# RWKV block inverse: the 16-step substitution as one run on GpSimd instead of portions on VectorE

## What is computed

```python
    def step(state, inp):
        rt, wt, kt, vt, at, bt = inp
        sa = jnp.einsum('bhvk,bhk->bhv', state, at)
        state = state * wt[:, :, None, :] + sa[..., None] * bt[:, :, None, :] + vt[..., None] * kt[:, :, None, :]
        return state, jnp.einsum('bhvk,bhk->bhv', state, rt)
```

## Time and profile before

| | |
|---|---|
| median of 3 runs | 1715.83 us (1714.31 to 1716.86) |
| the profiled execution | 1716.01 us, span 1713.9 us |
| TensorE | 1640.9 us busy, 96% of the span |
| VectorE | 1121.7 us, 65% |
| ScalarE | 874.3 us, 51% |
| GpSimd | 769.2 us, 45% |
| mean granted TensorE clock | 0.981 of 2.4 GHz |

### The profile page before, as it was taken

One profiled execution on the slowest core, in us unless ns is written; L12 is line 12 of the kernel. 1 busy time (PEld: TensorE's weight loads), 2 busy tenths in 40 slices (PEclk: granted clock), 3 DMA queues, 4 the chain that ended last, 5 costly groups with the idle time before them and its releaser, 6 DMA issues.

```text
span 1713.9 us, 30381 instructions
## 1 busy us (share of the span) xinstructions
PE 1640.9 (96%) x11876; PEld 1272.5 (74%) x11876; DVE 1121.7 (65%) x1732; ACT 874.3 (51%) x1695; POOL 769.2 (45%) x555
## 2 busy tenths in 40 slices
PE   8999999989888888899999999999999999999997
PEld 6677777745677677688977677788888888888886
DVE  8744343435576775633687769887758866784788
ACT  5323333345425444511463467776667666656763
POOL 4210212011111112312493257968768695867771
PEclk9999999988899999999999999999999999999999
DMA  6100010001112223322302002020211202020202
GB/s 242 37 26 22 25 47 1 22 6 31 33 32 49 52 36 116 140 107 73 111 25 74 1 1 98 21 79 25 74 36 63 70 30 96 29 74 26 74 1 98
DMA packets 82842, 94.47 MB, mean 55 GB/s; under 512 B 53776, under 2 KB 56336, under 8 KB 82704
## 3 DMA queue, kind: packets, MB, share of 16 engines
q1 hardware_dynamic: 82704, 92.57, 16.8%
HBM read 82.57 MB, written 9.98 MB: 54 GB/s over the span
## 4 chain that ended last, share of the span: by engine, by line
PE 78%; DVE 11%; ACT 4%; issue 3%; DMA 2%; POOL 2%; SPq 0%; DVEq 0%; ACTq 0%; POOLq 0%
PE PS L1763 40%; PE PS L1054 8%; PE PS L969 5%; PE PS L1155 3%; PE PS L1194 2%; PE PS L1173 2%; PE PS L1719 2%; PE PS L1697 1%; PE PS L1553 1%; PE PS L1228 1%; POOL sa L917 1%; DVE xn L2382 1%; PE PS L1395 1%; PE PS L1499 1%; DMA sc_s<-a_dram 1%
## 5 line engine op out<-in xcount | busy, mean ns | idle before, releaser
L1763 PE MATMUL PS<-memr,wsp 128*128 128x512 f32 x1488 | 357.6, 391 | 1.5 <-DVE memr L2952 1.5
L1763 PEld LDWEIGHTS PS<-memr,wsp 128*128 128x128 f32 x1488 | 278.8, 188 | 63.7 <-DVE memr L2952 3.7
L932 POOL TENSOR_TENSOR wsp<-sa,wsp 128x512 fp32r<-128x512 f32 x120 | 166.3, 1390 | 167.2 <-ACT wsp L2204 167.0
L1763 PE MATMUL PS<-memr,wraw_r 128*128 128x512 f32 x744 | 180.1, 390 | 0.4 <-DVE memr L2952 0.4
L1763 PEld LDWEIGHTS PS<-memr,wraw_r 128*128 128x128 f32 x744 | 139.4, 188 | 31.1 <-DVE memr L2952 1.2
L1054 PE MATMUL PS<-xn,wsp 128*128 128x512 f32 x576 | 147.8, 403 | 2.5 <-DVE proj L2427 1.6
L1763 PE MATMUL PS<-tmp_r,wsp 128*128 128x512 f32 x564 | 147.2, 395 | 2.6 <-DVE tmp_r L2952 2.2
L2952 DVE TENSOR_TENSOR memr<-PS,memr 128x512 fp32r<-128x512 f32 x185 | 126.2, 682 | 34.3 <-ACT PS L2242 34.3
L823 POOL CAST wsp<-wraw 128x1024 fp32r<-128x1024 f32 x24 | 27.9, 1161 | 239.2 <-PE PS L1054 114.2
L2970 DVE TENSOR_TENSOR H<-PS,H 128x512 f32<-128x512 f32 x160 | 108.2, 687 | 40.3 <-PE PS L1763 24.2
L1898 ACT ACTIVATE H<-PS,mst 128x128 f32<-128x128 f32 (+3 forms) x64 | 47.5, 742 | 166.1 <-DVE mst L2511 166.1
(11 more groups left out here) (394 smaller groups left out, 3437.0 us busy)
## 6 DMA issues: line engine op xcount, KB each, us to landing
sa<-in_weights_dram SPq DMA_DIRECT2D x40, 512.0 KB, 4.0
wraw<-in_weights_dram SPq DMA_DIRECT2D x24, 512.0 KB, 3.8
sa<-in_weights_dram SPq DMA_DIRECT2D x48, 256.0 KB, 2.6
H<-in_x_dram SPq DMA_DIRECT2D x16, 512.0 KB, 7.1
sbx<-in_weights_dram SPq DMA_DIRECT2D x32, 256.0 KB, 2.6
H<-in_weights_dram SPq DMA_DIRECT2D x8, 512.0 KB, 7.5
out_dram<-sbx SPq DMA_DIRECT2D x16, 256.0 KB, 2.1
a_dram<-H SPq DMA_DIRECT2D x16, 128.0 KB, 2.5
```

What stands on the lines that cost most here:

```text
L932: nc.gpsimd.tensor_tensor(w[:, 1, :], w_source(g), w[:, 0, :].bitcast(F32), ALU.subtract).then_inc(mw_rest, 1)
L1763: last = nc.tensor.matmul(PS[:, bank_of(g), :], w[:, a, win(k)], x[:, b, :], start=(k == 0 and (a, b) == (0, 0)), stop=(k == ROWS - 1 and ...
```

## The change

Places 24 and 26 to 30 leave VectorE. GpSimd gets place 24 (two memsets) and one place 26, in which all 15 steps and the transposed copy stand in one run; each of these instructions waits for the one before it on GpSimd's own counter `P_POOL`. SP waits for xt on that counter. Shapes, operands and operations stay the same.

```diff
-SUBST = {26: (0, 1, 2, 3), 27: (4, 5, 6, 7), 28: (8, 9, 10, 11), 29: (12, 13), 30: (14,)}
+SUBSTITUTE = 26
...
         P_DVE = Steps(sem("prep_dve"), each(
-            ["kk", "t1p", "L", "na", "am", "k2", "nkk", "at", "b", "bt", "kt", "al0", "al1", "al2", "al3", "rk", "x0", "x1"]
-            + [y for place in SUBST for j in SUBST[place] for y in (f"xm{j}", f"xa{j}")] + ["xt", "bv0", "bv1a", "bv1"]))
-        P_POOL = Steps(sem("prep_pool"), each(["rt", "kh", "bh"]))
+            ["kk", "t1p", "L", "na", "am", "k2", "nkk", "at", "b", "bt", "kt", "al0", "al1", "al2", "al3", "rk", "bv0", "bv1a", "bv1"]))
+        P_POOL = Steps(sem("prep_pool"), each(
+            ["rt", "kh", "bh", "x0", "x1"] + [y for j in range(BLK - 1) for y in (f"xm{j}", f"xa{j}")] + ["xt"]))
...
-                sp.wait_ge(P_DVE.sem, P_DVE.at(f"xt_{n}", -1))
+                sp.wait_ge(P_POOL.sem, P_POOL.at(f"xt_{n}", -1))
...
+                if s == 24:
+                    if n >= 1:
+                        pool.wait_ge(x_blocks_stored, 32 * n)
+                    nc.gpsimd.memset(bX, 0.0).then_inc(P_POOL.sem, P_POOL.one(f"x0_{n}"))
+                    own(f"x0_{n}")
+                    nc.gpsimd.memset(sc_s[:, 3456:3712:BLK + 1], 1.0).then_inc(P_POOL.sem, P_POOL.one(f"x1_{n}"))
+                if s == SUBSTITUTE:
+                    for j in range(BLK - 1):
+                        if j == 0:
+                            own(f"x1_{n}")
+                            pool.wait_ge(a_blocks_loaded, 16 * (n + 1))
+                        else:
+                            own(f"xa{j - 1}_{n}")
+                        shape = [P, BLK - 1 - j, j + 1]
+                        below, part = bX[:, j + 1:BLK, 0:j + 1], bT[:, j + 1:BLK, 0:j + 1]
+                        nc.gpsimd.tensor_tensor(part, bA[:, j + 1:BLK, j:j + 1].broadcast_to(shape),
+                                                bX[:, j:j + 1, 0:j + 1].broadcast_to(shape), ALU.mult).then_inc(
+                            P_POOL.sem, P_POOL.one(f"xm{j}_{n}"))
+                        own(f"xm{j}_{n}")
+                        nc.gpsimd.tensor_tensor(below, below, part, ALU.add).then_inc(P_POOL.sem, P_POOL.one(f"xa{j}_{n}"))
+                    own(f"xa{BLK - 2}_{n}")
+                    nc.gpsimd.tensor_copy(bXT, bX.rearrange("p i n -> p n i")).then_inc(P_POOL.sem, P_POOL.one(f"xt_{n}"))
...
-                if s in SUBST:
-                    for j in SUBST[s]:
...
-                        r(nc.vector.tensor_tensor(part, bA[:, j + 1:BLK, j:j + 1].broadcast_to(shape),
-                                                  bX[:, j:j + 1, 0:j + 1].broadcast_to(shape), ALU.mult), f"xm{j}")
-                        own(f"xm{j}")
-                        r(nc.vector.tensor_tensor(below, below, part, ALU.add), f"xa{j}")
-                if s == max(SUBST):
-                    own(f"xa{BLK - 2}")
-                    r(nc.vector.tensor_copy(bXT, bX.rearrange("p i n -> p n i")), "xt")
```

More of the change, by code:

```diff
@@ L847, in prep, with own @@
                 wt = rW.rearrange("p (c t) -> p c t", c=NC)[:, :, CH - 1:CH].broadcast_to([P, NC, CH])
+                def own(name):
+                    pool.wait_ge(P_POOL.sem, P_POOL.at(name, -1))
                 if s == 17:
```

## The result

The changed kernel took **1721.38 us** (median of 22 runs, 1712.87 to 1728.19) against 1714.82 (22 runs of the kernel before, beside it). The ratio is **1.0037, 95% interval [1.0025, 1.0049]**: slower by 0.37%, some 6.4 us.

The account below looks back on a forecast made before the run. Bound: VectorE's substitution holding up the loop, with X's own path to double_q close behind. Terms: -4.5 (attention end) + 2.25 (later double_q) + 4.5 (clock) = +2.25 us, so 1718 us; range 1709 to 1731.

Parts of the forecast that it names:

- the likeliest case: Whole kernel: GpSimd run of 10.1 to 12.4 us, tail won, rest given back; 1712 to 1720 us, chance 0.40.
- Parts 1 and 3: Third groups of the loop: about 15 us won over three pairs, then spent waiting for X before double_q.
- Part 2: Substitution on GpSimd: the run built from larger tiles, 11.1 us plus 0.9 for short rows, 12.0 us.
- Contention: VectorE and GpSimd slowing each other when both read SBUF: none seen during the run, so no price given.
- Part 3: X before double_q, pairs 1 to 3: X 9.1 us later in all, less slack, delays double_q by 2.25 us.
- Part 4: TensorE's clock behind the wait before double_q: nothing to 3.4 us a pair, 1.5 taken, +4.5 us in all.
- Part 5: End of the attention, pair 0: row maxima no longer wait behind VectorE's substitution portions; -4.5 us.
- The slower rival: GpSimd's run before double_q: steps twice VectorE's length, run 15.6 us, total +13 us, 1729 us; chance 0.40.
- Faster: GpSimd's run before double_q: 10 us or less, X about 1 us late, 1710 us; chance 0.20.

Follow-up runs that it names:

- e3_yn_waits: The changed kernel, with VectorE's steps yn and yb made to wait for the copy xt of pairs 2 and 3; 1.0007 [0.9989, 1.0025] against the kernel before.
- e1_pair0: The kernel before, with the substitution moved to GpSimd for pair 0 alone; 0.9966 [0.9949, 0.9983] against the kernel before.
- e2_pairs123: The kernel before, with the substitution moved to GpSimd for pairs 1 to 3 only; 1.0052 [1.0034, 1.0071] against the kernel before.
- e5_busy5: The changed kernel plus five filling TensorE products ahead of double_q of pairs 1 to 3; 1.0002 [0.9986, 1.0017] against the kernel before.
- e9_whole: The changed kernel measured once more, GpSimd for all four pairs; 1.0043 [1.0028, 1.0058] against the kernel before.
- e7_three: The changed kernel with yn waiting for xt, GpSimd's run ahead of kh and bh (pairs 1 to 3), and three filling TensorE products; 0.9979 [0.9964, 0.9995] against before.
- the repairs: The changed kernel with yn waiting for xt and GpSimd's run ahead of kh and bh: 0.9984; with three filling products too: 0.9979; both against the kernel before.

## Why the prediction was right, and which of its terms were off

The time lies in the range (1709 to 1731), the kernel is a little slower as forecast, and the mechanism is the one described: what the loop wins is spent in front of double_q, with the clock behind it. The sum was too small: +2.25 us was forecast, +6.4 measured, and the likeliest case, "within 0.2%", is missed (0.37% [0.25, 0.49]). That the range holds this is in part luck: its upper part was there for runs of 15.6 us, and those did not come.

- **Parts 1 and 3, the mechanism: right.** VectorE's work in the third group stopped holding the loop: from the landing of A to where TensorE has nothing left ahead of double_q the loop is 5.6, 4.5 and 5.2 us shorter, 15.3 in all, against the 15 forecast. The time was spent in front of double_q: 6.66, 5.24 and 7.89 us, where 5 to 7 were named. Of slack there were 6.94 us (6.85 read), and all of it was used up. The fourth group's dg stayed hidden, as costed: rMT of that group waits for TensorE or for VectorE's own queue.
- **Part 2, the run: right where it was alone.** Built from rows it came to 11.1, with 0.9 for short rows on top; measured it is 11.3 us for pairs 0 and 1, so at most 0.2 of that surcharge is borne out. The multiply of 64 elements took 0.31 us (0.275 by the sum), the add 0.32 (0.33). Over pairs 1 to 3 the runs sum to 37.0 us, against 36.0 forecast. That near hit is luck: a surcharge that did not exist stood in for a contention that had no price.
- **The term that was missing: *Contention*, "I give it no price".** The prediction looked at VectorE's instructions as they stood beside the substitution in the kernel before, where yn and yb came after it. But the change itself moves the loop forward and empties VectorE's queue, and that brings yn and yb, two SBUF inputs each, beside the end of the run in pairs 2 and 3. It cost 0.9 and 2.1 us of run length. e3_yn_waits takes this away and lands at 1.0007 [0.9989, 1.0025]; the forecast's +2.25 us (1.0013) lies in that interval, but so does no change. The prediction had looked for the right thing, VectorE instructions with more than one SBUF tile, but not at the time when they would run. What such a meeting costs stood in the trace of before, the other way round, in the timelines of VectorE and GpSimd:

```profile
500.56 0.22 DVE L2631 TENSOR_TENSOR sc_s<-sc_s 128x63 f32<-128x63 f32 x1
500.82 0.60 DVE L2634 TENSOR_TENSOR sc_s<-sc_s 128x63 f32<-128x63 f32 x1
...
500.73 1.18 POOL L902 TENSOR_TENSOR ssum<-con,rsm 64x256 f32<-64x256 f32 x2 [4.18 <-DVE ssum L2823]
```

  Beside dg, which had started 0.09 us ahead of it, an add of 63 elements takes 0.60 us; the add of as many 1.5 us earlier took 0.22.
- **Part 3, its size.** X later by 9.1 less a slack of 6.85 gave +2.25; measured it is 11.31 - 6.81 = +4.50. Contention put in 3.0 and a longer store 2.7 that had no term; the shorter run (2.0 over three pairs) and faster loads (1.28) took some back.
- **Part 4, the clock: right mechanism, too small.** +4.5 was taken from between 0 and 3.4 a pair; 6.86 was measured (2.75, 1.37 and 2.74), and 6.9 to 8.6 in the other kernels with a bare wait. Part of the low clock did lie inside the wait, as the prediction said (granted clocks of 0.61, 0.66 and 0.76 there). The forecast had 6.8 us at 1.2 GHz a pair in all; worked out from the granted clocks of the waits and of the stretches behind them it was some 10.3, 6.7 and 10.2 us, so more was left behind the wait than was put in.
- **Part 5, the end of the attention: right, somewhat too small.** -4.5 was forecast (bounds 3.5 and 6.9); e1_pair0 has it alone at -5.8 [-8.7, -2.9], the landing of pair 1's A at -6.7.
- **The rivals.** The slower rival's steps of twice VectorE's length, a run of 15.6 us, didn't come: 0.31 against 0.23 us for the steps of 64 elements, 11.3 us alone. The rule of the Trainium skill, GPSIMD Engine Reference, section "Performance versus the Vector engine", by which that rival held, does not fit tiles this small. *Faster*, a run of 10 us or less, was out by 1.3 us; the sum from rows, 11.1 without a surcharge, had not reached down to 10 either.

In one sum, against 1715: -6.7 + 4.5 + 6.8 = +4.6 at the end of the loop, and some 2 more from behind it in the profiles; the runs say +6.4 ± 2. The three terms were each too small by 2.2 to 2.4 us, one of them the gain, so their errors partly cancelled.

**What stays open.** The store of X took longer only for pairs 2 and 3, and its second DMA took long to issue on SP (row of the kernel after):

```profile
634.09 2.71 SPq L701 DMA_DIRECT2D xt_dram<-sc_s  x1
```

That is against 0.93 to 0.96 before. In all traces an issue over 1 us came only behind a copy that had been held up (after, e2_pairs123, e5_busy5, e9_whole), but not behind each of these; whether the one causes the other wasn't tried. Nor is the issue all of it: in e3_yn_waits the store of pair 2 took 5.9 us from the end of the copy to its landing with an issue of 0.94, where it was 5.4 after and 4.6 before. Also not settled is whether the products of e7_three are worth their own cost.

## What to carry to other kernels

Work that is taken off a full engine is worth only what the next releaser leaves, so measure the slack of the result's own path per stage first (landing of its input, landing of itself, start of its consumer). Here the gain came from the one instance whose result has cover (pair 0, 0.9966); the other three lost as changed, and even with the repairs (0.9984 and 0.9979) it is not shown that they gain anything on top of it. After such a move, lay the timelines of both engines over each other as they will stand, not as they stood: what the emptied queue brings forward may fall beside the moved work.

## What the runs showed of the hardware

- A GpSimd instruction whose tile has 15 elements a partition takes 0.21 to 0.24 us, one of 64 takes 0.31 to 0.33, and dependent ones stand 0.07 to 0.08 us apart; rows of 1 to 15 elements inside a tile cost next to nothing (11.3 us for the run, 11.1 by a sum without them). In these steps the part that does not grow with the tile is the larger one (0.16 to 0.19 us, an estimate from the sum of the prediction), and GpSimd takes 1.2 to 1.4 times what VectorE takes.
- GpSimd lost nearly all of the time that it stood beside a VectorE instruction with two SBUF inputs which had started first: 15 elements took 1.30 us instead of 0.22, a copy 1.49 and 1.66 instead of 0.61. An add on VectorE lost time the same way beside a GpSimd product that had started first (0.60 instead of 0.22).
- Waits of 5 to 8 us on TensorE in the kernel after were each followed by a stretch at a mean granted clock of 0.77 to 0.90, 1.4 to 2.8 us longer than at 1.00. A filling product of 128x512 in f32 took 0.88 us at a granted clock of 1.00.
